# A two-block transformer kernel: what its last combination waits for, and how the experts' gates are computed

## The chip, the cores and the metric

The kernel runs on one core of one Trainium2 chip. The core has five engines with instruction streams of their own: TensorE (PE, matrix products, with its weight loads shown as PEld), VectorE (DVE), ScalarE (ACT), GpSimd (POOL) and SyncE (SP), which here only issues DMA transfers and waits. They are ordered by semaphores. The metric is the time of one execution on the device in microseconds; lower is better. Everything is computed in float32.

## The reference, cut to what matters

The reference is a diffusion-style block (gated feed-forward, hybrid attention, gated feed-forward) and behind it a second block with 16 meta tokens, a gated linear attention, a latent attention and a mixture of experts. The change touches only the mixture of experts and what comes after it, for 512 tokens of width 1024:

```python
def hier_moe(u, wg, bg, we, be, w_gate, w_up, w_down):
    ...                                   # router: one group of 8, in it the best 2 of 8 experts, gates
    def expert_block(args):
        xb, e = args
        hdn = jax.nn.silu(xb @ w_gate[e]) * (xb @ w_up[e])     # [.., 1024] x [1024, 512]
        return hdn @ w_down[e]                                 # [.., 512] x [512, 1024]
    ys = lax.map(expert_block, (xs, block_expert)).reshape(n_slots, D)
    out = jnp.zeros((n_tok + 1, D), f32).at[slot_tok].add(ys.astype(f32) * slot_gate[:, None])[:n_tok]
    return out.reshape(B, L, D).astype(u.dtype)

    h = h + hier_moe(rmsnorm(h, ffn_norm[l]), ...)
    return rmsnorm(h, final_norm)[:, N_META:]
```

silu(z) is z times sigmoid(z). There are 64 experts with three float32 matrices of 2 MB each.

## The kernel before, in words

The first block, the attention parts of the second and the router come first and end at about 1717 us; nothing in them is changed. The router leaves tables in SBUF: which expert each block of up to 64 rows uses (`expert_ix`), which tokens are its rows (`tok_ix`), where its results go (`asg_ix`), and the number of pairs of blocks (`pairs_ix`; `n_pairs`, and `n_more`, which is one less).

Then comes the expert loop. Each engine has a loop of its own over pairs of blocks, blocks j = 0 and j = 1 with buffers of their own, and they meet by semaphores:

- SP reads gate, up and down weights (2 MB each, six ring slots, three for each j) by `gate_up_in` and `down_in`. It waits until PE has finished with the slot: `s_mg` and `s_mu` (gate and up projection done), `s_my` (down projection done).
- GpSimd gathers the 64 token rows of a coming block (`gather`, L2202) and scatters the 64 result rows of a finished one to `expert_rows` (`y_dram`) in HBM (`scatter`, L2217). Each scatter adds 16 to `s_scat[j]` when it has landed.
- PE turns the gathered rows (L1248), computes gate and up with the 64 rows stationary (`gate_up`, L1252 to L1268, 32 matmuls of 512 columns), turns the hidden rows (`turn_hidden`, L1274) and computes the down projection (`down`, L1285, 16 matmuls). Its order is written out: gate and up of the next block first, then the turning and the down projection of the block before. The last of the eight steps of gate and up waits for the hidden rows of the block before (`s_ha`).
- ScalarE copies the turned rows (L1602), takes exp(-z) of the gate projection (`gate_exp`, L1606), and copies the two halves of the result rows (`rows_out`, L1612).
- VectorE (`hidden`, L2144) adds 1 (L2147), takes the reciprocal (L2149), multiplies by z (L2151) and by the up projection (L2154), and copies the turned hidden rows (`hidden_in`, L2158).

In the last block PE first finishes the down projection of the block before, then waits for `s_ha` and issues one spare product (L1323) in front of the last transposes.

Behind the loop all four computing engines meet in `phase_end(.., 19)`: each issues a drain, adds one to a shared semaphore and waits until it stands at four. GpSimd comes there last, since it first waits for its own gathers and scatters and does one small addition (`settle(3)`). SP waits for the same semaphore (L680). Then SP issues the last reads: for each of four groups of 128 tokens both result rows, 1 MB (L683), and behind the first of them the final gain row, broadcast to 128 partitions, 0.5 MB (L685). VectorE adds the rows times their gates to the residual (L2183, L2185), ScalarE squares with a sum (L1639) and takes a square root (L1641), VectorE takes the reciprocal (L2176) and multiplies by it and the gain row (L2179), and SP writes the group out (L688). The computing engines meet once more in `phase_end(.., 22)`, and all five in the barrier of the block's end (L135).

Of the kernel before, what the change touches and what calls it, by code (L numbers as in the profile page):

```python
# [13 lines left out]
P = 128  # L14
# [118 lines left out]
def build(nc, a, out):  # L133
    ctx = ExitStack()
    with ctx:  # L135
# [3 lines left out]
        def sem(name):  # L139
            return ctx.enter_context(nc.semaphore(name))  # L140
# [268 lines left out]
        s_mg = sem("expert_gate_done")  # L409
        s_mu = sem("expert_up_done")  # L410
        s_my = sem("expert_down_done")
        s_eg = sem("expert_exp_ready")
        s_hd = sem("expert_hidden_ready")
        s_ha = sem("expert_hidden_rows_ready")
        s_ta = sem("expert_hidden_turned")
# [64 lines left out]
        def joined_count(n):  # L480
            return 4 * (JOINED.index(n) + 1) if n > LAST_LEFT else 4
# [48 lines left out]
        def _(sp):  # L530
# [138 lines left out]
            def down_in(j, block):  # L669
                e = sp.value_load(expert_ix[0:1, bass.ds(block, 1)], min_val=0, max_val=NE - 1)  # L670
                sp.wait_ge(s_my, block + 1)
                down_rows(j, e)
            with sp.Fori(2, n_pairs) as i:
                gate_up_in(0, i * 2)
                down_in(1, i * 2 - 1)
                gate_up_in(1, i * 2 + 1)
                down_in(0, i * 2)
            down_in(1, sp.snap(n_pairs * 2 - 1))

            sp.wait_ge(s_phase[LAST_LEFT + 1], joined_count(19))  # L680
            rows = y_dram.rearrange("(t p k) d -> t p k d", p=P, k=2)
            for t in range(NT):
                sp.dma_start(y2[t], rows[t]).then_inc(s_y2[t], 16)  # L683
                if t == 0:
                    sp.dma_start(gain_row, a["final_norm_2"].to_broadcast([P, D])).then_inc(s_row, 16)  # L685
            for t in range(NT):
                sp.wait_ge(s_fin, t + 1)
                sp.dma_start(out[0, t * P:(t + 1) * P, :], h2[:, t, :]).then_inc(s_out, 16)  # L688
# [4 lines left out]
        def _(pe):  # L693
# [629 lines left out]
            mm(ps[:, 7, 0:P], ident, ident, start=True, stop=True)  # L1323
            turn_hidden(1, None)
            down(1, before + 2, before16)
            phase_end(pe, 19)
            phase_end(pe, 22)


        @block.scalar  # L1330
        def _(act):
# [263 lines left out]
            av(rx[:, 0:NT * NG], rx[:, 0:NT * NG], ACT.Exp)  # L1595
            av(rx[:, NT * NG:NT * NG + NT], rx[:, NT * NG:NT * NG + NT], ACT.Exp).then_inc(s_rx, 1)

            act.drain().then_inc(s_ysf, 2)

            def rows_in(j, n):  # L1600
# [2 lines left out]

            def gate_exp(j, n):
                act.wait_ge(s_mg, n + 2)
                av(sg[j], ps[0:CAP, j, :], ACT.Exp, scale=-1.0).then_inc(s_eg, 1)  # L1606

            def rows_out(j, n):
                act.wait_ge(s_my, n + 2)
# [22 lines left out]
            gate_exp(1, before + 2)  # L1632
            rows_out(0, before + 1)
            rows_out(1, before + 2)
            phase_end(act, 19)
            for t in range(NT):

                act.wait_ge(s_y2f, t + 1)
                av(sq_row, h2[:, t, :], ACT.Square, accum_out=glst[:, 32 + t:33 + t]).then_inc(s_fsq, 1)  # L1639
                act.wait_ge(s_fsq, t + 1)  # L1640
                av(glst[:, 36 + t:37 + t], glst[:, 32 + t:33 + t], ACT.Sqrt, scale=1.0 / D, bias=eps_col[:, 0:1]).then_inc(s_fst, 1)  # L1641
            phase_end(act, 22)


        @block.vector
        def _(dve):
# [497 lines left out]
            def hidden(j, n, done):  # L2144

                dve.wait_ge(s_eg, n)
                v.tensor_scalar(sg[j], sg[j], 1.0, None, ALU.add).then_inc(s_vec, 1)  # L2147
                dve.wait_ge(s_vec, done + 1)
                v.reciprocal(sg[j], sg[j]).then_inc(s_vec, 1)  # L2149
                dve.wait_ge(s_vec, done + 2)  # L2150
                v.tensor_tensor(sg[j], ps[0:CAP, j, :], sg[j], ALU.mult).then_inc(s_vec, 1)  # L2151
                dve.wait_ge(s_vec, done + 3)
                dve.wait_ge(s_mu, n + 2)
                v.tensor_tensor(hrow[j], ps[CAP:2 * CAP, j, :], sg[j], ALU.mult).then_inc(s_ha, 1)  # L2154

# [3 lines left out]
            hidden(0, 1, at)  # L2159
            with dve.Fori(0, n_more) as i:  # L2160
                hidden_in(0, i * 2 + 1)
                hidden(1, i * 2 + 2, i * 6 + (at + 3))
                hidden_in(1, i * 2 + 2)
                hidden(0, i * 2 + 3, i * 6 + (at + 6))
            before = dve.snap(n_more * 2)
            hidden_in(0, before + 1)
            hidden(1, before + 2, dve.snap(n_more * 6 + (at + 3)))
            hidden_in(1, before + 2)
            phase_end(dve, 19)

            steps[0] = 0
            vec_sem[0] = s_vec2
# [14 lines left out]
                if t >= 1:  # L2187
                    final_row(t - 1)
            final_row(NT - 1)
            phase_end(dve, 22)  # L2190


        @block.gpsimd
        def _(pool):
            for n in tuple(range(1, LAST_LEFT + 1)) + tuple(m for m in JOINED if m <= 18):
                phase_end(pool, n)

            def settle(cell=0):

                return pool.tensor_tensor(spare[:, cell:cell + 1], spare[:, 2:3], spare[:, 2:3], ALU.add)  # L2200

            def gather(j, b, copies):  # L2202

                pool.tensor_copy(tcol[j][:, :], tok_ix[:, bass.ds(b, 1)]).then_inc(s_pix, 1)  # L2204
                pool.wait_ge(s_pix, copies)
                settle()
                pool.indirect_dma_start(xs[j], None, u_dram, bass.IndirectOffsetOnAxis(tcol[j][:, :], 0),
                                        bounds_check=SEQ - 1, oob_is_err=False).then_inc(s_gat[j], 16)
            pool.memset(spare[:, :], 0.0).then_inc(s_pix, 1)  # L2209
            pool.wait_ge(s_pix, 1)  # L2210
            pool.wait_ge(s_ud, 16 * NT)
            pool.wait_ge(s_pos, 3)
            pool.wait_ge(s_bet, 2)
            n_more = pool.value_load(pairs_ix[0:1, 1:2], min_val=2, max_val=MAX_PAIRS - 1)
            gather(0, 2, 2)
            gather(1, 3, 3)
            def scatter(j, b, copies, n, earlier):  # L2217

                if earlier is not None:
                    pool.wait_ge(s_scat[j], earlier)  # L2220
                    settle(1).then_inc(s_ysf, 1)
                pool.tensor_copy(acol[j][:, :], asg_ix[:, bass.ds(b, 1)]).then_inc(s_pix, 1)
                pool.wait_ge(s_pix, copies)
                pool.wait_ge(s_yc, n)
                settle()
                pool.indirect_dma_start(y_dram, bass.IndirectOffsetOnAxis(acol[j][:, :], 0), ys[j], None,
                                        bounds_check=N_ASG - 1, oob_is_err=False).then_inc(s_scat[j], 16)

            for j in range(2):
                pool.wait_ge(s_xt, j + 3)  # L2230
                gather(j, j + 4, 2 * j + 4)
                scatter(j, j, 2 * j + 5, j + 1, None)
            with pool.Fori(1, n_more) as i:
                for j in range(2):
                    pool.wait_ge(s_xt, i * 2 + (j + 3))
                    gather(j, i * 2 + (j + 4), i * 4 + (2 * j + 4))
                    scatter(j, i * 2 + j, i * 4 + (2 * j + 5), i * 2 + (j + 1), i * 16)
            before = pool.snap(n_more * 2)
            for j in range(2):
                scatter(j, before + j, pool.snap(n_more * 4 + (j + 4)), pool.snap(n_more * 2 + (j + 1)), pool.snap(n_more * 16))  # L2240
            for j in range(2):
                pool.wait_ge(s_gat[j], pool.snap(n_more * 16 + 16))
                pool.wait_ge(s_scat[j], pool.snap(n_more * 16 + 16))
            settle(3)
            for n in (m for m in JOINED if m >= 19):
                phase_end(pool, n)


_INS = ["x", "w_mod", "w1_gate", "w1_up", "w1_down", "w_in", "b_f", "w_o", "w2_gate", "w2_up", "w2_down", "meta_tokens_2",
# [21 lines left out]
```

## Time and profile before

| | us |
|---|---|
| median of 3 runs | 2755.42 |
| lowest, highest | 2754.99, 2758.76 |
| span of the profiled execution | 2753.4 |

The page gives no other time of the profiled execution than its span.

| engine | busy us | share of the span |
|---|---|---|
| PE | 2477.8 | 90% |
| DVE | 1050.1 | 38% |
| ACT | 478.7 | 17% |
| POOL | 177.2 | 6% |

The shares are means over stages that differ. The expert loop, from about 1725 us to the end, is moved by another resource than the first 1700 us, as the slices of the page show. In a timeline row the first number is the start in us from the beginning of the span, the second how long it took; the bracket at its end says how long the engine had been idle before and what released it. "SPq" and "POOLq" are the instruction streams of SP and GpSimd, where DMA issues, drains and register work are recorded.

### The profile page before, as it was taken

The page shows a single profiled execution, that of the slowest core. Times are in us where ns is not written, and L with a number is a line of the kernel's source. Part 1 is how long each engine was busy: PE and PEld are TensorE (multiplying, and loading weights), DVE is VectorE, ACT ScalarE, POOL GpSimd, SP SyncE. Part 2 cuts the span into 40 slices and gives each one's busy share as a digit, 9 for nine tenths or more (in the row PEclk, how much of TensorE's full clock was granted, in tenths as well). Part 3 has the DMA queues.
Part 4 walks back from the last instruction along what each step waited for, and adds up shares of the span by engine and source line. Part 5 has one row for each costly group of instructions (what it writes and reads, how often), then busy time and mean ns, then how long its engine had stood idle before and what let it go on. Part 6 is the DMA issues. An engine that isn't in the chain of part 4 may idle for free. (4 is left out here: it accounts for less than half of the span.)

```text
span 2753.4 us, 24397 instructions
## 1 busy us (share of the span) xinstructions
PE 2477.8 (90%) x8987; PEld 1142.8 (42%) x8987; DVE 1050.1 (38%) x1244; ACT 478.7 (17%) x751; POOL 177.2 (6%) x452
## 2 busy tenths in 40 slices
PE   8999999999899999999899998988888878888783
PEld 4444444466564444444354554333333323333231
DVE  3555540144553333330133725433333333333333
ACT  2000000156341100000021321111111111111111
POOL 0000000000000000000000000111111111111110
PEclk9999999999899999999999999998999999999997
DMA  7443644011201122422401022999999999999994
GB/s 279 149 145 132 212 134 109 23 46 47 85 1 61 56 66 64 119 53 63 139 22 36 31 107 115 375 419 415 416 407 412 406 413 404 410 407 413 405 417 168
DMA packets 182671, 563.08 MB, mean 205 GB/s; under 512 B 16732, under 2 KB 132716, under 8 KB 156384
## 3 DMA queue, kind: packets, MB, share of 16 engines
q1 hardware_dynamic: 172384, 554.10, 52.6%
q0 software_dynamic: 10240, 8.31, 1.0%
q8 instruction: 35, 0.57, 0.1%
q14 instruction: 12, 0.10, 0.0%
HBM read 566.66 MB, written 20.97 MB: 213 GB/s over the span
## 5 line engine op out<-in xcount | busy, mean ns | idle before, releaser
L1266 PE MATMUL ps<-slot,xT 128*64 128x512 f32 x2048 | 511.2, 657 | 152.8 <-DMA slot<-in_expert_w_up 150.0
L770 PE MATMUL ps<-hT,slot 128*128 128x512 f32 x1408 | 615.3, 598 | 12.9 <-ACT hT L1370 7.2
L770 PEld LDWEIGHTS ps<-hT,slot 128*128 128x128 f32 x1408 | 267.8, 191 | 351.9 <-issue 348.4
L1266 PEld LDWEIGHTS ps<-slot,xT 128*64 128x64 f32 x2048 | 155.5, 150 | 505.4 <-issue 299.9
L799 PE MATMUL ps<-big,slot 128*128 128x512 f32 x704 | 306.0, 594 | 3.3 <-issue 2.9
L2158 DVE COPY hT<-ps 128x256 f32<-128x256 f32 x64 | 27.2, 425 | 616.9 <-PE ps L1274 616.9
L1285 PE MATMUL ps<-slot,hT 128*64 128x512 f32 x1024 | 235.5, 602 | 1.8 <-DVE hT L2158 1.8
L2149 DVE RECIPROCAL xT<-xT 64x512 f32<-64x512 f32 x64 | 214.1, 3345 | 2.2
L799 PEld LDWEIGHTS ps<-big,slot 128*128 128x128 f32 x704 | 132.4, 190 | 176.1 <-issue 176.1
L1733 DVE RECIPROCAL eb<-eb 128x512 f32<-128x512 f32 x44 | 147.5, 3353 | 1.5
L1731 DVE TENSOR_SCALAR eb<-eb 128x512 f32<-128x512 f32 x44 | 18.8, 427 | 332.6 <-ACT eb L1380 332.6
L1606 ACT ACTIVATE xT<-ps 64x512 f32<-64x512 f32 x64 | 37.8, 591 | 583.1 <-PE ps L1266 583.1
L1285 PEld LDWEIGHTS ps<-slot,hT 128*64 128x64 f32 x1024 | 68.9, 137 | 116.6 <-issue 112.5
L1612 ACT ACTIVATE hT<-ps 64x512 f32<-64x512 f32 x128 | 75.8, 592 | 198.4 <-PE ps L1285 197.6
L1757 DVE SCALAR_TENSOR_TENSOR xT<-ps,small,xT 128x512 f32<-128x512 f32 x16 | 12.0, 750 | 250.8 <-PE ps L799 250.7
L821 PE MATMUL ps<-hT,slot 128*128 128x512 f32 x240 | 105.9, 597 | 0.0
L1380 ACT ACTIVATE eb<-ps 128x512 f32<-128x512 f32 x44 | 26.3, 597 | 419.5 <-PE ps L770 419.4
L2209 POOL MEMSET spare<- 1x4 f32 x1 | 0.1, 92 | 1379.0 <-ACTq L486 1379.0
L1357 ACT ACTIVATE tmp<-xT 128x512 f32<-128x512 f32 (+1 forms) x32 | 20.1, 632 | 334.3 <-DVE xT L1757 298.6
L2204 POOL COPY tcol<-tok_ix 64x1 int32 (+1 forms) x64 | 11.4, 178 | 909.7 <-PE ps L1248 559.7
L827 PE MATMUL ps<-slot,hT 128*128 128x128 f32 x512 | 61.8, 284 | 6.9 <-DVE big L1821 6.9
L821 PEld LDWEIGHTS ps<-hT,slot 128*128 128x128 f32 x240 | 44.9, 190 | 55.2 <-issue 55.2
(353 smaller groups left out, 2325.0 us busy)
## 6 DMA issues: line engine op xcount, KB each, us to landing
slot<-in_expert_w_gate SPq DMA_DIRECT2D x64, 2048.0 KB, 17.1
slot<-in_expert_w_up SPq DMA_DIRECT2D x64, 2048.0 KB, 22.4
slot<-in_expert_w_down SPq DMA_DIRECT2D x64, 2048.0 KB, 22.8
slot<-in_w_mod SPq DMA_DIRECT2D x18, 2048.0 KB, 8.1
slot<-in_w_gate SPq DMA_DIRECT2D x22, 1024.0 KB, 5.5
slot<-in_w_up SPq DMA_DIRECT2D x22, 1024.0 KB, 7.9
slot<-in_w_down SPq DMA_DIRECT2D x16, 1408.0 KB, 8.1
slot<-in_w_in SPq DMA_DIRECT2D x24, 512.0 KB, 6.2
```

The source lines that it names most:

```text
L770: last = mm(ps[:, 2 * j + g, :], w[:, g, k, j * P:(j + 1) * P], hT[:, k, META:TOK], start=(k == 0), stop=(k == KC - 1))
L799: last = mm(ps[:, down_bank(d), :], w[:, f, :], aT[:, f, :], start=(f == 0), stop=(f == FC - 1))
L821: last = mm(ps[:, bank, :], pair_w[p][:, k, m, :], hT[:, k, META:TOK], start=(k == 0), stop=(k == KC - 1))
L827: last = mm(ps[:, bank, t * P:(t + 1) * P], hT[:, k, META + t * P:META + (t + 1) * P], pair_w[p][:, k, 2, :], start=(k == 0), stop=(k == K ...
L1266: last = mm(ps[g * CAP:(g + 1) * CAP, j, :], xsT[j][:, k, :], w[g][:, k, :], start=(k == 0), stop=(k == KC - 1))
L1285: last = mm(ps[g * CAP:(g + 1) * CAP, 2 + j, :], hid[j][:, c, :], w[:, c, g * 512:(g + 1) * 512], start=(c == 0), stop=(c == 3))
L1380: av(eb[:, j, :], ps[:, 2 * j, :], ACT.Exp, scale=-1.0).then_inc(s_ge, 1)
L1606: av(sg[j], ps[0:CAP, j, :], ACT.Exp, scale=-1.0).then_inc(s_eg, 1)
L1612: last = av(ys[j][:, g * 512:(g + 1) * 512], ps[g * CAP:(g + 1) * CAP, 2 + j, :], ACT.Copy)
L1733: v.reciprocal(eb[:, j, :], eb[:, j, :]).then_inc(s_vec, 1)
L2149: v.reciprocal(sg[j], sg[j]).then_inc(s_vec, 1)
L2158: v.tensor_copy(hid[j].rearrange("p c s -> p (c s)"), ps[:, 6 + j, 0:4 * CAP]).then_inc(s_hd, 1)
```

## The change

Four edits, all in the second half of the kernel:

1. SP no longer waits for the phase semaphore in front of the last reads but for the two scatter semaphores. Phases 19 and 22 are gone from PE, ScalarE, VectorE and GpSimd.
2. The final gain row is read before SP's loop over the weights, behind the down weights of block 2, instead of between the last reads.
3. The gate is one sigmoid on ScalarE. The addition and the reciprocal on VectorE go, and the counts of `s_vec` follow.
4. A sigmoid of one column is issued on ScalarE in front of the loop, behind the router's exponentials.

```diff
+            sp.dma_start(gain_row, a["final_norm_2"].to_broadcast([P, D])).then_inc(s_row, 16)
             with sp.Fori(2, n_pairs) as i:
                 gate_up_in(0, i * 2)
                 down_in(1, i * 2 - 1)
...
             down_in(1, sp.snap(n_pairs * 2 - 1))
 
-            sp.wait_ge(s_phase[LAST_LEFT + 1], joined_count(19))
+            for j in range(2):
+                sp.wait_ge(s_scat[j], sp.snap(n_pairs * 16))
             rows = y_dram.rearrange("(t p k) d -> t p k d", p=P, k=2)
             for t in range(NT):
                 sp.dma_start(y2[t], rows[t]).then_inc(s_y2[t], 16)
-                if t == 0:
-                    sp.dma_start(gain_row, a["final_norm_2"].to_broadcast([P, D])).then_inc(s_row, 16)
...
-            phase_end(pe, 19)
-            phase_end(pe, 22)
...
+            av(fox_s[:, 15:16], eps_col[:, 0:1], ACT.Sigmoid)
             act.drain().then_inc(s_ysf, 2)
...
-                av(sg[j], ps[0:CAP, j, :], ACT.Exp, scale=-1.0).then_inc(s_eg, 1)
+                av(sg[j], ps[0:CAP, j, :], ACT.Sigmoid).then_inc(s_eg, 1)
...
-            phase_end(act, 19)
...
-            phase_end(act, 22)
...
                 dve.wait_ge(s_eg, n)
-                v.tensor_scalar(sg[j], sg[j], 1.0, None, ALU.add).then_inc(s_vec, 1)
+                v.tensor_tensor(sg[j], ps[0:CAP, j, :], sg[j], ALU.mult).then_inc(s_vec, 1)
                 dve.wait_ge(s_vec, done + 1)
-                v.reciprocal(sg[j], sg[j]).then_inc(s_vec, 1)
-                dve.wait_ge(s_vec, done + 2)
-                v.tensor_tensor(sg[j], ps[0:CAP, j, :], sg[j], ALU.mult).then_inc(s_vec, 1)
-                dve.wait_ge(s_vec, done + 3)
                 dve.wait_ge(s_mu, n + 2)
                 v.tensor_tensor(hrow[j], ps[CAP:2 * CAP, j, :], sg[j], ALU.mult).then_inc(s_ha, 1)
...
-            phase_end(dve, 19)
...
-            phase_end(dve, 22)
...
             settle(3)
-            for n in (m for m in JOINED if m >= 19):
-                phase_end(pool, n)
```

## Rows read from the trace of the kernel before

**Rows 1.** The page: what the DMA engines moved, in 40 equal slices.
```profile
GB/s 279 149 145 132 212 134 109 23 46 47 85 1 61 56 66 64 119 53 63 139 22 36 31 107 115 375 419 415 416 407 412 406 413 404 410 407 413 405 417 168
```

**Rows 2.** Waits of 1750 to 2680 us: us in total, times, longest us.
```profile
PE ps L1266 <- DMA slot<-in_expert_w_up: 148.9, 53, 4.7
```

**Rows 3.** Weight issues of 1762 to 2670 us, their register step: ns, first and last start.
```profile
L626 SPq FUSED_REGOPS  x59: 37/37/37, 1762.9 to 2669.7; - x59
```

**Rows 4.** Timeline of PE: hidden rows turned, in two successive blocks.
```profile
1762.77 0.69 PE L1274 MATMUL ps<-cst,hT 64*128 64x64 f32 x4
...
1774.73 0.69 PE L1274 MATMUL ps<-cst,hT 64*128 64x64 f32 x4
```

**Rows 5.** Timeline of the last block, 2700 to 2708 us.
```profile
2700.39 0.59 ACT L1606 ACTIVATE xT<-ps 64x512 f32<-64x512 f32 x1 [6.90 <-PE ps L1266]
...
2701.36 0.41 DVE L2147 TENSOR_SCALAR xT<-xT 64x512 f32<-64x512 f32 x1
2701.59 3.65 PE L1285 MATMUL ps<-slot,hT 128*64 128x512 f32 x16 [0.61 <-DVE hT L2158]
2701.80 3.35 DVE L2149 RECIPROCAL xT<-xT 64x512 f32<-64x512 f32 x1
...
2705.99 0.69 DVE L2154 TENSOR_TENSOR hT<-ps,xT 64x512 f32<-64x512 f32 x1
...
2706.74 0.49 PE L1323 MATMUL ps<-cst 128*128 128x128 f32 x2 [1.49 <-DVE hT L2154]
...
2707.36 0.93 POOL L2226 DMA_INDIRECT expert_rows<-hT,acol  x1 [0.55 <-issue]
```

**Rows 6.** Timeline between the last scatter and the first read.
```profile
2714.20 0.91 POOL L2226 DMA_INDIRECT expert_rows<-hT,acol  x1 [0.52 <-issue]
2716.88 0.18 POOL L2200 TENSOR_TENSOR spare<-spare 1x1 f32<-1x1 f32 x1 [1.77 <-DMA expert_rows<-hT,acol]
2727.62 0.33 SPq L683 DMA_DIRECT2D slot<-expert_rows  x1
```

**Rows 7.** GpSimd's instructions of L486 in 2700 to 2726 us: min/median/max ns.
```profile
L486 POOLq DRAIN  x1: 10744/10744/10744, 2716.8 to 2716.8; - x1
```

**Rows 8.** Waits of SP from 1650 us on.
```profile
SPq L683 <- POOLq L486: 35.0, 1, 35.0
```

**Rows 9.** DMA issues of 2714 to 2717 us, with the median us to landing.
```profile
expert_rows<-hT,acol POOLq DMA_INDIRECT x1, 2.5
```

**Rows 10.** The four reads of result rows (L683), starts and landings.
```profile
L683 SPq DMA_DIRECT2D slot<-expert_rows x4: 331/452/727, 2727.6 to 2729.7; - x4
...
DMA to landing us min/median/max: 4.8/9.4/12.1
```

**Rows 11.** The landing of the up weights issued at 1725.1 us.
```profile
DMA to landing us min/median/max: 13.1/13.1/13.1
```

**Rows 12.** Timeline of the last combination: the second group of rows and the first root.
```profile
2736.42 1.28 ACT L1641 ACT_TABLE_LOAD   x1
2736.89 1.28 DVE L2183 SCALAR_TENSOR_TENSOR big<-slot,gates,big 128x1024 f32<-128x1024 f32 x1 [1.73 <-DMA slot<-expert_rows]
2737.71 0.29 ACT L1641 ACTIVATE glst<-glst,eps_col 128x1 f32<-128x1 f32 x1
...
2739.41 0.16 DVE L2176 RECIPROCAL glst<-glst 128x1 f32<-128x1 f32 x1
```

**Rows 13.** The barrier of the block's end, GpSimd's drain: min/median/max ns.
```profile
L135 POOLq DRAIN  x1: 34/34/34, 2750.6 to 2750.6; - x1
```

**Rows 14.** Timeline of PE at the loop's start.
```profile
1734.42 1.08 PE L1266 MATMUL ps<-slot,xT 128*64 128x512 f32 x4 [1.35 <-DVE hT L2154]
```

**Rows 15.** Timeline of ScalarE between router and loop.
```profile
1691.95 1.28 ACT L1595 ACT_TABLE_LOAD   x1
1700.43 0.23 ACT L1595 ACTIVATE hT<-hT 128x32 f32<-128x32 f32 x1 [7.20 <-DVE hT L2065]
...
1711.73 0.60 ACT L1616 ACTIVATE xT<-ps 128x512 f32<-128x512 f32 x1 [10.97 <-PE ps L1228]
```

More of the change, by code:

```diff
@@ L411, in build @@
         s_my = sem("expert_down_done")
-        s_eg = sem("expert_exp_ready")
+        s_eg = sem("expert_sigmoid_ready")
         s_hd = sem("expert_hidden_ready")
@@ L2161, in _ @@
                 hidden_in(0, i * 2 + 1)
-                hidden(1, i * 2 + 2, i * 6 + (at + 3))
+                hidden(1, i * 2 + 2, i * 2 + (at + 1))
                 hidden_in(1, i * 2 + 2)
-                hidden(0, i * 2 + 3, i * 6 + (at + 6))
+                hidden(0, i * 2 + 3, i * 2 + (at + 2))
             before = dve.snap(n_more * 2)
             hidden_in(0, before + 1)
-            hidden(1, before + 2, dve.snap(n_more * 6 + (at + 3)))
+            hidden(1, before + 2, dve.snap(n_more * 2 + (at + 1)))
             hidden_in(1, before + 2)
-            phase_end(dve, 19)
             steps[0] = 0
```

## The prediction

> **What bounds the kernel now.** I read the slices of the page first: from the 27th of the 40 to the 39th the DMA engines move 404 to 419 GB/s [rows 1]. That is the expert loop, 64 blocks of three 2 MB weight tiles. The waits of 1750 to 2680 us say who waits for whom: 53 times PE idles until up weights have landed [rows 2]. SP's issues give the pace: the 59 blocks issued from 1762.9 to 2669.7 are 58 steps of 906.8 / 58 = 15.63 us [rows 3]. Where the weights are already there, a block of PE's takes 1774.73 - 1762.77 = 11.96 us [rows 4]. So the stream of weights sets the loop, each block has 3.67 us of slack for everything else, and an edit inside the loop counts only at its two ends. Behind the loop no weights move: the rows from 2714 us on show a chain of scatter, GpSimd, SP, row reads, combination and write [rows 6, 8, 12]. A microsecond out of that chain is one out of the kernel.
>
> **Part 1: the barrier in front of the reads.** The last scatter is issued at 2714.20 and lands 2.5 us later, at 2716.7 [rows 6, 9]. GpSimd goes on at 2716.88, and then its DRAIN in phase 19 takes 10,744 ns, up to about 2727.6 [rows 7]. SP's wait is put down to just that, and SP issues the first read at 2727.62 [rows 6, 8]. In the changed kernel SP waits for the two scatter semaphores instead. Both count 16 a pair, so n_pairs x 16 is the last scatter of either buffer; nothing is queued behind SP's wait but the reads. GpSimd's own answer to that landing takes 0.18 us; I give SP, which needs no arithmetic first, 0.1: 2716.8. Removed: 2727.62 - 2716.8 = **10.8 us**. The bounds are 0 (something else holds the reads, rival 1) and 10.9. The kernel's final barrier takes over a drain of GpSimd. Even if that one lasts 10.7 us it ends near 2728, while SP waits for the last output write until the end of the span; that wait is the cover, and without it the gain would be gone. Phase 22, behind the final rows, does not hold SP, so it is worth 0.
>
> A page would price the drain otherwise. The Trainium skill, "VectorE: DVE Perf Modes", section "The DRAIN you can't avoid", tells of drains of about 12 ns on all five engines around a kernel. GpSimd's drain in this kernel's final barrier is of that kind, 34 ns [rows 13]; the one at 2716.8 is not. If a drain were always that cheap, the 10.7 us would belong to another event and could stay.
>
> **Part 2: sigmoid for exp, add and reciprocal.** Per block VectorE loses an add of 0.41 us and a reciprocal of 3.35. The sigmoid has the shape of the exponential, 64x512, 0.59 us [rows 5]. The trace shows no sigmoid; I bound its difference by -0.6 and +1.3 (nothing, and a table load beside it) and take 0, the nearest row being the exponential's. In the loop the gain is hidden under the weight wait. In the last block not quite: PE ends the down projection of the block before at 2701.59 + 3.65 = 2705.24 and waits until 2706.74 for the hidden rows, which VectorE ends at 2705.99 + 0.69. Without the two operations two products of some 0.69 remain, and the rows are ready at 2701.36 + 2 x 0.69 = 2702.7, before PE is [rows 5]. What is late next is PE's own down projection, so of 3.8 us only 2706.74 - 2705.24 = **1.5 us** come off, and all that follows (transposes, last down projection, copy, scatter) moves with it. GpSimd doesn't hold it up: its scatter before the last one is issued at 2707.36 and takes 0.93, done 5.9 us before the last [rows 5, 6]. A sigmoid 1.3 us longer would still have them ready at 2704.0; the bounds are 0 (PE meets another wait there) and 1.5.
>
> The dummy sigmoid in front of the loop adds a table load of 1.28 us and an activation of at most 0.6. ScalarE's exponential there is at 1700.43 and its next work at 1711.73, behind 10.97 us of idling [rows 15], so it costs 0; without that cover, 1.9. The final square root has its own load before and after.
>
> **Part 3: the gain row.** Its read of 0.5 MB leaves the place between the first and the second row read. Before, the first read landed at 2727.62 + 4.8 = 2732.42 and the second just before 2736.89; VectorE idled 1.73 us for it, from 2735.16 [rows 10, 12]. The fourth, issued at 2729.7, landed 12.1 later, 2741.8, so a read of 1 MB takes (2741.8 - 2736.9) / 2 = 2.5 us [rows 10]. With nothing between, the second lands at 2734.9, before VectorE ends the first combination (2735.16). The chain then goes over ScalarE: its table load starts at 2736.42 whatever VectorE does, its root ends at 2737.71 + 0.29 = 2738.00, and the first reciprocal follows at 2738.03 instead of 2739.41 [rows 12]. That is 1.38 us less. The third read (2737.4 on these clocks) is needed at about 2739.4, and the later rows are paced by VectorE. I take **1.3**, with bounds 0 and 1.7, the whole idle time.
>
> The read isn't free where it goes: SP issues it behind the down weights of block 2, into a queue that already holds the stream. At 410 GB/s 0.52 MB are 1.3 us, by which the gate weights behind it land later. Against it stands what the stream may gain at its start: PE idles 1.35 us for the first hidden rows at 1734.42 [rows 14], which now come in time, so the next issues go out up to 1.35 us earlier. That helps only if the DMA engines ran dry there. The up weights issued at 1725.14 landed 13.1 us later, at 1738.2, behind PE's rows of 1734.42 + 1.08 = 1735.50, which free the slots for the next issue [rows 11, 14], so the slowest engine was never idle, and the slowest sets a landing. I take **+1.3**, bounds -0.1 and +1.3.
>
> **Sum.** -10.8 - 1.5 - 1.3 + 1.3 = -12.3 us. The span of 2753.4 becomes 2741.1. The page gives the profiled execution's span and no other time; the median of the runs, 2755.42, stands 2.0 above it, and I carry those 2.0 over: **2743.1 us**.
>
> **Rivals.** (1) The 10.7 us stay: they are not the drain's but the time until something in the chip lets written rows be read or GpSimd's queue go, and the new wait or the first read takes them on. For it: the other drain of GpSimd is short [rows 13]. Against it: the drain has its own record, and it begins after the landing was already reported. Time: 2755.42 - 1.5 = **2753.9**, no difference that can be told. The page of part 1 speaks for this one.
> (2) The start of the loop counts: its 1.35 us take the gain row's place in the stream. 2743.1 - 1.35 = **2741.7**.
> (3) Slower: on ScalarE sigmoid and copy need different tables, and each of the four activations of a block (sigmoid, xT copy, two ys copies) reloads on PE's path. A load is 1.28 us [rows 12]: 11.96 + 4 x 1.28 = 17.08 us a block, 1.45 over the stream's 15.63, times 60 = 87: **2830 us**. It decides from 3.67 + 12.3 / 60 = 3.88 us a block on the path, just over three loads; two loads stay hidden and cost some 1.3 at the tail (2744.4). Against it: a load runs ahead of its activation's wait (1691.95 against 1700.43) [rows 15], and PE's path has to wait for only one of the four, the xT copy.
> By the Trainium skill, "ScalarE: Activation LUTs", section "Table sets: the hidden batching unit", copy stands in every set, so no load would come. By its section "What ACT_TABLE_LOAD costs" a switch is about 2.66 us with its drain; two a block, all on the path, would be 17.28 us and slower. No row of before shows a sigmoid.
>
> **Chances.** Forecast 0.77, rival 2 0.14, rival 1 0.05, rival 3 0.02, and 0.02 for a slower stream or clock for reasons I don't see. The range takes in the bounds of the stream (-1.4), the tail (-0.4 to +1.3), a table load at the tail (+1.3) and a microsecond of scatter between medians: 2739.5 to 2746.5. A measurement of this kernel can tell about 0.2%, 5.5 us. Faster by more: 0.92 (forecast, rival 2, and 0.01 of the last case); within: 0.05; slower: 0.03.
>
> **What would show it.** Right: SP's first read within 0.3 us of the last scatter's landing; PE no longer idle in front of the last transposes for hidden rows; the second row read landing some 2.5 us behind the first, and ScalarE's root in front of the first reciprocal; a GpSimd drain of some 10 us beside the reads; one table load more in front of the loop and none in it; weights of the last block up to 1.3 us later. Wrong: a gap between landing and first read, a last output write followed by a wait for GpSimd, table loads in the loop, a pace away from 15.6 us a block.

## The result, and the profile after

| | us |
|---|---|
| changed kernel, first series: median of 4 runs (lowest, highest) | 2738.74 (2738.27, 2739.55) |
| before, beside it: median of 4 runs | 2755.2 |
| ratio (changed over before), 95% interval | 0.9941 [0.9927, 0.9956] |
| forecast (range) | 2743.1 (2739.5 to 2746.5) |
| span of the profiled execution, before and after | 2753.4, 2736.5 |

The kernel became faster, as forecast, but by 16.5 us where 12.3 were forecast, and the median lies 0.8 us below the range. Two more series of the same changed kernel gave 2743.81 (5 runs) and 2742.86 (6 runs), ratios 0.9955 [0.9942, 0.9969] and 0.9951 [0.9937, 0.9964]. All 15 runs together have a median of 2741.6 (2736.6 to 2746.3), 80 runs of the kernel before, taken from all series, 2755.0 (2751.3 to 2762.1): 13.4 us.

The two first profiles, cut at instructions that both have, show where their -16.9 us lie: -5.6 ahead of the expert stream, where nothing was changed; +2.5 in the loop; -1.6 in the last block; -10.8 between the last scatter and the first read; -1.4 behind it. The rows of the profile after, in the order of the forecast's steps. First the pace of the loop, as start of SP's register step in front of each gate read, and PE's waits of 1750 to 2665 us:

```profile
L626 SPq FUSED_REGOPS  x60: 37/37/48, 1742.0 to 2666.5; - x60
```
```profile
PE ps L1266 <- DMA slot<-in_expert_w_up: 147.8, 51, 4.7
```

(2666.5 - 1742.0) / 59 = 15.67 us a block, against 15.63 [rows 3], and PE idles for the up weights as it did [rows 2]: the stream still sets the loop. The timeline of the last block, for [rows 5]:

```profile
2697.30 0.59 ACT L1605 ACTIVATE xT<-ps 64x512 f32<-64x512 f32 x1 [5.90 <-PE ps L1266]
...
2698.27 0.67 DVE L2144 TENSOR_TENSOR xT<-ps,xT 64x512 f32<-64x512 f32 x1
2698.50 3.65 PE L1285 MATMUL ps<-slot,hT 128*64 128x512 f32 x16 [0.61 <-DVE hT L2151]
2699.07 0.69 DVE L2147 TENSOR_TENSOR hT<-ps,xT 64x512 f32<-64x512 f32 x1
2702.08 0.49 PE L1323 MATMUL ps<-cst 128*128 128x128 f32 x2
```

The sigmoid takes the exponential's 0.59 us, the hidden rows are ready at 2699.76, and PE goes from its projection to the spare product with no idle time. Next the scatter, the first read and GpSimd's drain (start, us; and ns in the drain's row), for [rows 6, 7]:

```profile
2709.55 0.91 POOL L2217 DMA_INDIRECT expert_rows<-hT,acol  x1 [0.52 <-issue]
2712.14 1.99 SPq L685 DMA_DIRECT2D slot<-expert_rows  x4
2712.22 0.18 POOL L2191 TENSOR_TENSOR spare<-spare 1x1 f32<-1x1 f32 x1 [1.76 <-DMA expert_rows<-hT,acol]
```
```profile
L135 POOLq DRAIN  x1: 10744/10744/10744, 2712.2 to 2712.2; - x1
```

The first read is issued 0.08 us before GpSimd wakes on the same landing. The drain is as long as before to the nanosecond, but belongs to the final barrier now and is over at 2722.9, 13.6 us before the end. The last combination, for [rows 12]:

```profile
2719.58 1.28 DVE L2175 SCALAR_TENSOR_TENSOR big<-slot,gates,big 128x1024 f32<-128x1024 f32 x1
...
2720.86 1.28 ACT L1639 ACT_TABLE_LOAD   x1
...
2722.16 0.29 ACT L1639 ACTIVATE glst<-glst,eps_col 128x1 f32<-128x1 f32 x1
...
2722.49 0.16 DVE L2168 RECIPROCAL glst<-glst 128x1 f32<-128x1 f32 x1 [0.31 <-ACT glst L1639]
```

VectorE no longer waits for the second rows, and the first reciprocal waits for ScalarE's root, as forecast. In front of the loop the early sigmoid lies in ScalarE's idle time, for [rows 15]:

```profile
1694.92 1.28 ACT L1596 ACT_TABLE_LOAD   x1
...
1696.22 0.20 ACT L1596 ACTIVATE fox_s<-eps_col 128x1 f32<-128x1 f32 x1
...
1706.13 0.60 ACT L1615 ACTIVATE xT<-ps 128x512 f32<-128x512 f32 x1 [9.71 <-PE ps L1228]
```

The loads of ScalarE from 1720 us on, by group, are one:

```profile
L1639 ACT ACT_TABLE_LOAD x1 | 1.3, 1283 | 0.0
```

### The profile page after: what moved, and what is told of

It is laid out like the page before. It is cut to its first block, busy times and chain, and to the rows that moved or that the text cites. A ratio compares the mean times of both kernels' runs of the same rounds, so it can differ in the third digit from the quotient of the medians.

```text
span 2736.5 us, 24133 instructions
## 1 busy us (share of the span) xinstructions
PE 2473.8 (90%) x8987; PEld 1140.9 (42%) x8987; DVE 809.2 (30%) x1116; ACT 480.0 (18%) x753; POOL 177.5 (6%) x452
## 4 chain that ended last, share of the span: by engine, by line
PE 68%; DMA 24%; DVE 4%; issue 2%; ACT 1%; SPq 1%; POOL 0%; POOLq 0%; DVEq 0%; ACTq 0%
DMA slot<-in_expert_w_up 24%; PE ps L770 22%; PE ps L799 11%; PE ps L1266 11%; PE ps L821 4%; PE ps L1183 2%; PE ps L912 2%; PE ps L988 2%; PE ps L827 2%; PE ps L986 1%; PE ps L983 1%; PE ps L845 1%; PE ps L872 1%; PE ps L1128 1%; DVE eb L1822 1%
## 5 line engine op out<-in xcount | busy, mean ns | idle before, releaser
L1248 PE MATMUL ps<-cst,xT 64*128 64x64 f32 x496 | 64.9, 271 | 0.0
```

Of the source, the lines that this page charges most:

```text
L1248: last = nc.tensor.transpose(ps[:, 4 + j, k * CAP:(k + 1) * CAP], xs[j].rearrange("p (m k) -> p k m", k=KC)[:, k, :], ident[0:CAP, 0:CAP])
```

## The experiments

All 20 profiles, us. "Ahead": to the issue of the up weights of block 2. "Loop": from there to the first gate matmul of the last block but one. "Last block": first gate matmul to last scatter. "Gap": to the first read. "Tail": to the end of the span. The last block but one, between loop and last block, has 14.96 to 15.05 us in every profile.

| kernel | ahead | loop | last block | gap | tail | span |
|---|---|---|---|---|---|---|
| before | 1725.1 | 953.2 | 20.9 | 13.4 | 25.8 | 2753.4 |
| before_again | 1719.7 | 955.2 | 22.6 | 13.4 | 25.9 | 2751.9 |
| wait_alone | 1719.4 | 953.5 | 23.9 | 2.6 | 26.0 | 2740.4 |
| gain_alone | 1720.7 | 955.8 | 24.3 | 13.4 | 24.3 | 2753.5 |
| sigmoid_alone | 1720.2 | 953.0 | 21.0 | 13.4 | 25.8 | 2748.4 |
| after | 1719.5 | 955.7 | 19.4 | 2.6 | 24.4 | 2736.5 |
| after_2nd | 1725.9 | 955.7 | 21.1 | 2.6 | 24.3 | 2744.5 |
| after_3rd | 1724.3 | 955.3 | 19.4 | 2.6 | 24.1 | 2740.7 |
| exp_restored | 1724.5 | 955.4 | 24.3 | 2.6 | 24.2 | 2746.0 |
| gain_restored | 1724.7 | 954.1 | 19.4 | 2.6 | 25.7 | 2741.4 |
| barrier_no_drain | 1721.6 | 953.6 | 23.9 | 2.9 | 25.9 | 2742.9 |
| drain_early | 1725.6 | 954.4 | 22.6 | 12.0 | 25.8 | 2755.4 |
| idle_added | 1720.9 | 954.3 | 22.2 | 2.6 | 24.3 | 2739.2 |
| wait_filled | 1719.7 | 954.5 | 22.6 | 2.6 | 24.3 | 2738.7 |
| busy_added | 1726.1 | 955.2 | 20.3 | 2.6 | 24.1 | 2743.3 |
| busy_added_2nd | 1720.0 | 955.5 | 20.3 | 2.6 | 24.2 | 2737.6 |
| busy_added_3rd | 1719.0 | 954.8 | 20.3 | 2.6 | 24.3 | 2736.0 |
| gain_in_gap | 1718.8 | 954.4 | 19.4 | 2.6 | 24.2 | 2734.4 |
| gain_in_gap_2nd | 1719.4 | 953.1 | 20.9 | 2.6 | 24.2 | 2735.3 |
| best | 1725.5 | 954.2 | 19.4 | 2.6 | 24.4 | 2741.1 |

**Does the stretch ahead of the loop belong to the change?** before_again is the kernel before with no edit.

> The kernel before, unchanged, profiled a second time. In the two first profiles the stretch ahead of the expert stream (up to the issue of the up weights of block 2) took 1725.1 us before and 1719.5 after, though no instruction that acts there differs. Theory A (scatter): that stretch moves by several us between executions of one program, with the stretches at half clock, so this profile can lie anywhere from 1719 to 1726, and the span with it from 2748 to 2756. Theory B (the change did it, say by the layout of the code): this profile gives 1725 within 1 us and 2753 to 2754.

Measured: 2753.77 us (10 runs, 2752.3 to 2759.5), ratio 0.9997 [0.9987, 1.0007]. SP's row, to be set against the 1725.1 of [rows 11], and the windows of 900 to 950 and 1550 to 1600 us, before and again (us, busy of PE, PEld, DVE, ACT, POOL, granted clock, DMA share, GB/s):

```profile
1719.72 0.43 SPq L626 DMA_DIRECT2D slot<-in_expert_w_up  x1
```
```profile
900.00:950.00 50.00, 49.66 (x112) 21.63 (x111) 16.25 (x15) 7.31 (x10) 0.00 (x0) 0.96 0.13 42
1550.00:1600.00 50.00, 48.48 (x244) 30.54 (x242) 27.98 (x67) 18.26 (x52) 0.00 (x0) 0.97 0.00 1
```
```profile
900.00:950.00 50.00, 49.66 (x116) 21.77 (x115) 15.48 (x12) 4.39 (x6) 0.00 (x0) 1.00 0.13 42
1550.00:1600.00 50.00, 48.48 (x253) 31.33 (x252) 27.22 (x72) 20.17 (x59) 0.00 (x0) 1.00 0.00 1
```

Theory A holds: the kernel before, without an edit, needed 5.4 us less there in this execution than in the first. A part is TensorE's clock: PE is as busy in both windows and gets fewer matmuls done (112 against 116, 244 against 253) in the profile in which the clock stood at 1.2 GHz for a part of them. Over all 20 profiles the stretch lies at 1718.8 to 1721.6 (twelve) or 1724.3 to 1726.1 (eight), with edits and without, and the time that TensorE's granted clock was at 1.2 GHz in it parts them without an exception: 78.5 us in each of the twelve, 81.9 to 92.2 us in the eight (85.3 in before). That isn't all of it. 6.8 us more at half clock can cost 3.4 us, not 5.4, and where the rest comes from is not shown. The chip isn't excluded as a part of it: the six profiles of one chip are all short, while each of three other chips has both kinds.

**The wait.** wait_alone takes edit 1 only.

```diff
-            sp.wait_ge(s_phase[LAST_LEFT + 1], joined_count(19))
+            for j in range(2):
+                sp.wait_ge(s_scat[j], sp.snap(n_pairs * 16))
...                                   # and no phase 19, 22
```

> Only edit 1: SP waits for the two scatter semaphores, phases 19 and 22 gone; exponential and gain row as before. By my sum: last scatter to first read 2.6 instead of 13.4 us, everything else as before, -10.8 us in all. Rival (drain's time moves on): the gap stays at 10 us or more, or the tail grows by as much. The tail from the first read to the end should stay 25.8, the last block 13.5 from its first matmul to the turning.

Measured: 2743.37 us (6 runs), ratio 0.9959 [0.9946, 0.9971] to before's 2756.0. By the profile the gap is 2.6 us, 10.8 less than before's 13.4, and the tail gives nothing back (26.0 for 25.8). The medians differ by 12.6, 1.8 more than the gap gives, which is within their scatter. barrier_no_drain keeps the barrier and takes only GpSimd's drain out of it:

```diff
-            settle(3)
-            for n in (m for m in JOINED if m >= 19):
-                phase_end(pool, n)
+            settle(3).then_inc(s_phase[LAST_LEFT + 1], 1)
+            pool.wait_ge(s_phase[LAST_LEFT + 1], joined_count(19))
+            phase_end(pool, 22)
```

> The kernel before with its barrier kept: SP still waits until the shared semaphore of phase 19 stands at four, and PE, ScalarE and VectorE still drain and meet there. Only GpSimd's share is signalled by its small addition behind the landed scatter, without a drain; its drain comes with phase 22. If the drain alone holds SP: last scatter to first read 2.9 us instead of 13.4, and the median as that of wait_alone, 11 us below before. If the meeting itself costs, the gap stays above 5 us.

```profile
2714.12 0.91 POOL L2226 DMA_INDIRECT expert_rows<-hT,acol  x1 [0.52 <-issue]
2716.80 0.18 POOL L2200 TENSOR_TENSOR spare<-spare 1x1 f32<-1x1 f32 x1 [1.77 <-DMA expert_rows<-hT,acol]
2717.01 0.33 SPq L683 DMA_DIRECT2D slot<-expert_rows  x1
```

A gap of 2.89 us: the meeting of four engines costs 0.3 us, the drain the other 10.5. Median 2744.44, ratio 0.9967 [0.9955, 0.9979]. drain_early adds `pool.drain()` to that kernel, directly behind the last scatter.

> barrier_no_drain with one more drain of GpSimd directly behind the issue of the last scatter, in front of its wait for the landing. If the drain's 10.74 us are a cost of their own, they run from 0.9 us behind the scatter's start, cover the landing, and the first read follows the last scatter by 11.9 to 12.5 us. If the drain waits for something that the landing ends, the first read follows by about 3 us. The second drain, of phase 22, should show whether each drain behind a scatter costs that or only the first (34 to 41 ns).

```profile
2717.61 0.91 POOL L2226 DMA_INDIRECT expert_rows<-hT,acol  x1 [0.52 <-issue]
2729.36 0.18 POOL L2200 TENSOR_TENSOR spare<-spare 1x1 f32<-1x1 f32 x1 [10.84 <-issue]
2729.57 0.34 SPq L683 DMA_DIRECT2D slot<-expert_rows  x1
```
```profile
L2241 POOLq DRAIN  x1: 11666/11666/11666, 2717.4 to 2717.4; - x1
```
```profile
L486 POOLq DRAIN  x1: 41/41/41, 2729.6 to 2729.6; - x1
```

The drain's record starts here before the scatter's instruction is over, and the drain ends 10.5 us behind the end of that instruction (2717.4 + 11.67 against 2717.61 + 0.91). In the kernel before it starts when the rows have landed, beside the small addition, and ends 10.5 us behind the end of the addition (2716.8 + 10.74 against 2716.88 + 0.18) [rows 6, 7]. So it is a cost of its own, counted from GpSimd's last instruction, and no wait for the landing. The next drain takes 41 ns: it is paid once. What in GpSimd's work brings it is not shown. Ahead of its earlier, short drains GpSimd did no work but a few MEMSETs; ahead of this one lie the 128 indirect DMAs of the loop, but its copies and small additions too. The addition alone doesn't bring it, since the drain of 41 ns stands behind one. Median 2754.7, ratio 0.9998 [0.9988, 1.0008].

**Sigmoid and gain row, alone and taken back.** sigmoid_alone and gain_alone are edits 3 and 4, and edit 2, on the kernel before; exp_restored and gain_restored undo the same on the changed one; after_2nd is the changed kernel with no edit, beside these two.

> Only edits 3 and 4: one sigmoid for exponential, addition and reciprocal, and the early sigmoid. By my sum: -1.5 us in the last block (13.5 to 11.9), 0 in the loop if the slowest DMA engine never idles, down to -1.35 if the early issue counts. Rival: the early issue is worth more than that, because PE also loses a stretch at half clock there, -3 us or more.

> Only edit 2: the gain row read in front of the loop. By my sum: tail 25.8 to 24.4 us, loop +1.3, together 0. The after trace has the loop 2.5 us longer: if the gain row costs all of that here, 2.5 is its price; if this loop is +1.3 or less, the rest is scatter or the sigmoid's.

> The changed kernel, unchanged, timed and profiled again. Theory A (the excess over the forecast is scatter of the stretch ahead of the loop and of the half-clock stretches): the runs spread as those of before do, over some 8 us, their median comes to 2740 to 2743, 13 to 15 us below before. Theory B (the edits are worth 16.5 us): the median stays within a microsecond of 2738.7.

> The changed kernel with exponential, addition and reciprocal again (edits 3 and 4 undone). By my sum 1.5 us slower than the changed kernel, in the last block alone (11.9 to 13.5 us). Rival that came up with the single edits: PE's wait for the hidden rows goes together with further half-clock stretches in the last two blocks, as in wait_alone and gain_alone (from the last gate matmuls to the last scatter 23.9 and 24.3 us against 19.4 in the changed kernel), then 3 to 5 us slower.

> The changed kernel with the gain row read again between the first and the second row read. By my sum 0.0 (tail +1.3, loop -1.3). If the loop gives back more than the bytes cost (953 to 954 instead of 955.7 us from the first up issue to the last gate but one), up to 1 us faster than the changed kernel.

| kernel | median, us (runs) | before | ratio |
|---|---|---|---|
| sigmoid_alone | 2752.18 (10) | 2756.0 | 0.9993 [0.9983, 1.0002] |
| gain_alone | 2755.18 (10) | 2756.0 | 1.0002 [0.9991, 1.0013] |
| exp_restored | 2747.76 (9) | 2754.59 | 0.9968 [0.9958, 0.9978] |
| gain_restored | 2742.40 (5) | 2754.59 | 0.9951 [0.9938, 0.9965] |

after_2nd gave the 2743.81 us of the section on the result, 5.1 above the first series and 0.8 above the band of theory A: theory B is out. The gain row comes out as 0 either way, within the scatter: gain_restored lies 1.4 us below after_2nd. The sigmoid's worth is more than 1.5 us: 4.0 between the medians of exp_restored and after_2nd. The table has it in the last block: 23.2 us in the mean of the seven profiles with the exponential alone (20.9 to 24.3), 20.0 in the eight with the sigmoid alone (19.4 to 21.1).

**What the other 1.7 us are.** Two stretches that are in part at half clock. The 32 gate and up matmuls of the last block take 7.09 us or 8.4 to 8.8, in after and before_again:

```profile
2690.18 7.09 PE L1266 MATMUL ps<-slot,xT 128*64 128x512 f32 x32
```
```profile
2689.94 8.78 PE L1266 MATMUL ps<-slot,xT 128*64 128x512 f32 x32 [2.84 <-DMA slot<-in_expert_w_up]
```

They are slow in 8 of the 12 profiles in which PE idled 2.8 us in front of them for the weights, and in none of the 8 in which it idled 1.4 or less. That goes with the stream and not with an edit: five of the eight are kernels with the exponential, three with the sigmoid, and this uneven draw makes 0.5 us of the 3.2. The rest is the last down projection: in most kernels in which PE waits for the last hidden rows, its 16 matmuls take 5.3 us and not 3.65. idle_added makes the rows late again though the sigmoid stays, by reciprocals whose result nobody reads; wait_filled fills most of that wait by spare products; busy_added delays the changed kernel's last projection by work.

```diff
+                v.reciprocal(unused, sg[j]).then_inc(s_vec, 1)      # idle_added, in hidden()
+                dve.wait_ge(s_vec, done + 1)
...
             down(0, before + 1, before16)                          # wait_filled: 3, busy_added: 4
+            for _ in range(3):
+                mm(ps[:, 7, 0:P], ident, ident, start=True, stop=True)
```

> The changed kernel, with one reciprocal into an unused tile in front of VectorE's two products, so that the hidden rows are late again by 3.35 us though sigmoid stays. By my first sum 1.0 us slower in the last block (PE idles again), else nothing. Theory of the second half-clock stretch: four of six kernels in which PE idles 1.49 us in the last block had a half-clock stretch in the last down projection (5.3 us instead of 3.65), none of the four in which it does not; if idling brings it, it comes back here in about two profiles of three.

> exp_restored with three spare products of the identity on PE in front of its wait for the last hidden rows, so that PE works through most of the 1.49 us. Its time on the path doesn't change, as it would wait anyway. If idling brings the second half-clock stretch, the last down projection takes 3.65 us here and the last block 20.9 or 22.6 us in all instead of 24.3, and the median lies 1 us or so below exp_restored's 2747.8. If the stretch has nothing to do with it, it shows up here as often.

> The changed kernel with four spare products of the identity on PE between its last two down projections, about 1.3 us of work and no idling, so that the last projection starts as late as with the exponential. If the half-clock stretch in the last projection belongs to PE's idling, the projection takes 3.65 us and the last block 20.7 us; if it belongs to the later position, it takes 5.3 us, 22.4 us in all. Either way the path is at least 1.3 us longer than the changed kernel's.

> Idling: no half clock in the last down projection, 3.65 us. Position: 5.3 us in about seven of nine such profiles.

> As busy_added_2nd. If all three profiles have 3.65 us, position alone would have given that with a chance of (2/9) to the third power, one in ninety.

PE's rows of the spare product and the last projection, in exp_restored, idle_added, wait_filled and busy_added:

```profile
2710.05 0.49 PE L1323 MATMUL ps<-cst 128*128 128x128 f32 x2 [1.49 <-DVE hT L2150]
...
2711.77 5.35 PE L1285 MATMUL ps<-slot,hT 128*64 128x512 f32 x16 [0.61 <-DVE hT L2154]
```
```profile
2703.19 0.49 PE L1323 MATMUL ps<-cst 128*128 128x128 f32 x2 [1.04 <-DVE hT L2151]
...
2704.91 5.35 PE L1285 MATMUL ps<-slot,hT 128*64 128x512 f32 x16 [0.61 <-DVE hT L2155]
```
```profile
2702.65 0.49 PE L1325 MATMUL ps<-cst 128*128 128x128 f32 x2 [0.63 <-DVE hT L2152]
...
2704.37 5.35 PE L1285 MATMUL ps<-slot,hT 128*64 128x512 f32 x16 [0.61 <-DVE hT L2156]
```
```profile
2709.22 0.39 PE L1325 MATMUL ps<-cst 128*128 128x128 f32 x2
...
2710.83 3.65 PE L1285 MATMUL ps<-slot,hT 128*64 128x512 f32 x16 [0.61 <-DVE hT L2153]
```

And the windows of that projection, exp_restored and busy_added (columns as above; the third from the right is the clock). The slow projection isn't at half clock throughout: of its 5.35 us some 3.4 are.

```profile
2713.00:2716.50 3.50, 3.50 (x11) 1.07 (x8) 0.00 (x0) 0.00 (x0) 0.00 (x0) 0.56 0.00 0
```
```profile
2711.50:2714.50 3.00, 2.99 (x14) 0.86 (x10) 0.00 (x0) 0.00 (x0) 0.17 (x2) 1.00 0.10 21
```

Of nine profiles with PE idle in front of the spare product, seven have the slow projection; of eleven without, none. All but one of the nine compute the exponential; the one that has the idling with the sigmoid, idle_added, has the slow projection too. In idle_added it starts 6.4 us behind the start of the one before; in busy_added, fast in three profiles of three, 6.2. So it goes with the idling and hardly with the position. 0.63 us of idling left, as in wait_filled, was enough once, so my expectation of wait_filled failed. What in the chip ties the two is not shown. Medians: idle_added 2742.94, wait_filled 2744.08, busy_added 2744.85 us; between kernels so near to one another these tell nothing.

**A better place for the gain row.** gain_in_gap reads it between the gate weights of block 1 and SP's wait for the first projection, where the DMA engines stand still.

```diff
             gate_or_up(1, 0, 1)
+            sp.dma_start(gain_row, a["final_norm_2"].to_broadcast([P, D])).then_inc(s_row, 16)
```

> The changed kernel, the gain row read where the DMA engines stand still: behind the gate weights of block 1 and ahead of SP's wait for the first gate projection. The windows of before show 0 GB/s from 1710 to 1725 us there. Theory (what the gain row costs in the loop is its bytes and its place in the queue): loop 953.0 to 954.1 us as in the kernels that read it behind the loop, tail 24.2 to 24.4 us, so about 1.9 us faster than the changed kernel. Rival (the longer loop of the four kernels with the moved read is chance): loop 955 or more.

> gain_in_gap again, on the same chip as after_3rd. Its read is off the weight stream, worth 1.3 us by the bytes, so the median should lie 0 to 3 us below after_3rd, and the loop at 953 to 954.5 us. If it lies above, the difference between the two can't be told from scatter.

> The changed kernel a third time. If the first series (2738.7) was a low draw, the median comes to 2740 to 2744 with a spread of 6 to 8 us, and the stretch ahead of the loop again lies at 1719 to 1721 or 1724 to 1726 us; if the second was the odd one, it stays at 2738 to 2740. The last block: 19.4 or 21.1 us from the last gate matmul to the last scatter, no half clock in the last down projection.

Measured: 2737.21 us (4 runs), ratio 0.9938 [0.9922, 0.9955], and 2740.14 (6 runs), 0.9947 [0.9933, 0.9961], beside after_3rd's 2742.86. The tail stays at 24.2 and the loops are 954.4 (0.3 above what I expected) and 953.1 us, 1.7 less in the mean than the 955.5 of the three profiles of the changed kernel. The median of its ten runs, 2737.3, is the lowest of all versions, but the lead of 2.7 us over the changed kernel in the one common series is within the scatter of medians. That this version is faster is not shown; the loop alone speaks for it.

> gain_in_gap with three more edits of the tail: a square root of one column on ScalarE in front of the last combination, so that its table load lies in the wait for the reads; the first 1 MB read split in two, so that VectorE starts when 0.5 MB are there; the last product and its write split in two halves of 512 columns. From the tail of the changed kernel, 24.3 us: the first chain is 0.6 us shorter (its second group is there 7.3 us behind the issue and no load stands before the root), the last write can start 0.6 us earlier. I expect 23.1 us, and the median 3 us below the changed kernel's. Rival: the split write costs as much at its second half (2.6 us behind the last product), tail 23.7.

best measured 2743.52, ratio 0.9955 [0.9937, 0.9972], and its tail is 24.4, not 23.1 us. Its rows say why:

```profile
2720.84 1.28 DVE L2186 SCALAR_TENSOR_TENSOR big<-slot,gates,big 128x1024 f32<-128x1024 f32 x1 [12.59 <-DMA slot<-expert_rows]
2722.40 1.28 DVE L2190 SCALAR_TENSOR_TENSOR big<-slot,gates,big 128x1024 f32<-128x1024 f32 x1 [0.27 <-DMA slot<-expert_rows]
...
2724.89 1.29 DVE L2186 SCALAR_TENSOR_TENSOR big<-slot,gates,big 128x1024 f32<-128x1024 f32 x1 [1.21 <-DMA slot<-expert_rows]
```

VectorE starts 0.8 us earlier behind the first read (4.1 instead of 4.9), but then waits 1.21 us for the second group: it is there 8.2 us behind the first read, where the changed kernel's was there by 7.4. What was saved at the front is paid one step later. Whether the extra issue or the smaller pieces delay it isn't shown.

## Why the prediction was right or wrong

**Where the miss lies.** 4.4 us lie between the forecast and the first series, 4.6 between the forecast span (2741.1) and the span measured beside it (2736.5). By the two profiles: -5.6 ahead of the loop, where I had put nothing, +1.2 in the loop (2.5 for 1.3), and at most 0.1 in each of the last block, the gap and the tail.

**The range: the step that failed.** I gave scatter "a microsecond", from three runs, and took the stretch ahead of the loop over from one profile as if it were fixed. It has two levels 5 us apart without an edit, and that profile had the upper one (1725.1), the first profile after the lower (1719.5). The medians of three series of the changed kernel were 2738.7, 2742.9 and 2743.8 us, so scatter between medians is 5 us and not 1. The forecast, 2743.1, is within 0.7 us of the two higher ones. The first was low: its profile has the lower level ahead and the shortest last block. That its other three runs, all within 1.3 us, had the lower level too is inferred from their times, as they have no profile; and which chip ran this series is not on record. The range is also not the sum that it names: -1.4 - 0.4 - 1 from 2743.1 is 2740.3, not 2739.5.

**Part 2, the last block: a term put too small.** This is the part of the miss that an edit makes. I put "only 2706.74 - 2705.24 = 1.5 us" and had PE's matmuls unchanged behind it. The wait of 1.5 is there and goes; but the means of the last block differ by 3.2 us. Of these 1.2 are the projection's: 8.65 us from the spare product to the scatter in the mean of the seven with the exponential, 7.47 in each of the eight with the sigmoid. It runs in part at half clock behind the idling in most executions. 0.5 more is the chance draw of the gate and up matmuls. The profile I worked from had neither: it was one of the two of nine with a fast projection behind idling, 20.9 us against a mean of 23.2, so no row of it could show the term. In the first two profiles the term therefore came out as forecast, 1.55 us, and adds nothing to their miss. With 1.5 + 1.2 = 2.7 in place of 1.5 the sum is -13.5 us, 2741.9, next to the 2741.6 of the 15 runs.

**The stream bounds the loop: right.** PE's waits and the pace stand. Neither four fewer microseconds of VectorE per block nor the early end of PE's first wait (1.35 us) shows in the loop: 954.0 us in five profiles with the exponential, 953.8 in five with the sigmoid, where the gain row is not in the stream and the loop scatters from 953.0 to 955.2. So rival 2 is out, though its 2741.7 us is as near to the median of all 15 runs as any number here: that is chance.

**Part 1, the barrier: right,** 10.83 us for 10.8. Rival 1 is out, by wait_alone and barrier_no_drain. The page that spoke for it (the Trainium skill, "VectorE: DVE Perf Modes", section "The DRAIN you can't avoid") tells of some 12 ns for the drains around a kernel. The short drains of GpSimd here, 34 and 41 ns, are of that order; its first one behind the loop's indirect DMAs is not.

**Part 3, the gain row: right in the sum.** The tail gave 1.6 us (25.8 to 24.2, in the means) for the forecast 1.3, and the ten profiles with the read in the stream have a loop of 955.2 us, the ten others 953.9: 1.3, as the bytes say. That the profile after shows +2.5 is 1.3 and the scatter of the loop.

**Rival 3 is out.** One load in front of the loop and none in it; so here "ScalarE: Activation LUTs" of the Trainium skill, section "Table sets: the hidden batching unit", agrees: copy stands in sigmoid's set too.

## What to carry to other kernels

A drain of GpSimd behind a loop of indirect DMAs is worth a look of its own wherever a barrier stands in front of transfers: wait for the landings and leave the drain to where something else covers it, as the combination did here. An edit that ends an idling of PE in a stretch bound by PE may give back more than the wait, because here the matmuls behind it kept the higher clock. And before a range is drawn from one profile, ask which of its stretches would look otherwise in the next execution: here those ahead of the loop and at its end, by 5 and 3 us.

## What was not expected of the hardware

GpSimd's first drain behind the scatters lasts 10.744 to 10.747 us in 18 of the 20 profiles, 10.518 in barrier_no_drain and 11.666 in drain_early. The three lengths are one: the drain's record can start before the instruction ahead of it is over, and the drain's end lies 10.53 us behind the end of that instruction in 19 profiles and 10.55 in barrier_no_drain. Nine earlier drains of GpSimd in the profile of before take 34 ns each. TensorE ran a part of the last projection at 1.2 in place of 2.4 GHz in 7 of 9 profiles after 0.6 to 1.5 us without work in front of the spare product, and in none of 11 in which only the usual 0.6 us behind the last transposes was idle; and a part of the last gate and up matmuls in 8 of 12 profiles after 2.8 us without work, and in none of 8 after 1.4 or less. Ahead of the loop, where nothing was edited, it stood at 1.2 GHz for 78.5 us in twelve profiles and for up to 92.2 in the others, and all of these others are the slower ones there.
